# Who scales the sub-layer outputs by the inverse root: VectorE and GpSimd together, or VectorE alone

## The reference

```
x = x + 0.5 * rmsnorm(swiglu(rmsnorm(x, n[0]), w1_gu[l], w1_down[l]), n[1])      # q = 0
m, S_a, S_r = mixer(rmsnorm(x, n[2]), pos, w_in[l], ..., w_out[l], ...)
x = x + rmsnorm(m, n[3])                                                         # q = 1
x = x + 0.5 * rmsnorm(swiglu(rmsnorm(x, n[4]), w2_gu[l], w2_down[l]), n[5])      # q = 2

rmsnorm(x, g) = x * rsqrt(mean(x * x) + 1e-6) * g
```

## Time and profile before

| | us |
|---|---|
| three runs | 2445.9, 2448.19, 2452.44 |
| their median | 2448.19 |
| the profiled execution's own time | 2452.13 |
| its span, first to last instruction | 2450.3 |
| TensorE busy | 2334.9 (95%) |
| VectorE busy | 814.8 (33%) |
| ScalarE busy | 865.8 (35%) |
| GpSimd busy | 999.2 (41%) |

### The profile page before, as it was taken

One profiled execution on the slowest core, in us unless ns is written; L12 is line 12 of the kernel. 1 busy time (PEld: TensorE's weight loads), 2 busy tenths in 40 slices (PEclk: granted clock), 3 DMA queues, 4 the chain that ended last, 5 costly groups with the idle time before them and its releaser, 6 DMA issues.

```text
span 2450.3 us, 44621 instructions
## 1 busy us (share of the span) xinstructions
PE 2334.9 (95%) x17793; PEld 2260.2 (92%) x17793; DVE 814.8 (33%) x1065; ACT 865.8 (35%) x1396; POOL 999.2 (41%) x814
## 2 busy tenths in 40 slices
PE   8999999899989899999889999989998989999998
PEld 7999999799877899999879999988998779999997
DVE  4222200687434522210142221015864344222102
ACT  4333333442312433333343333334423234333322
POOL 3444444544113544444434444444442044444443
PEclk9999999899989999999989999999999899999999
DMA  5322232232304123322223332223223132222231
GB/s 159 90 86 86 73 90 75 73 87 63 94 24 120 53 86 89 91 71 87 76 70 87 90 89 74 84 67 87 78 70 80 40 103 69 86 86 86 78 88 60
DMA packets 382847, 198.44 MB, mean 81 GB/s; under 512 B 6853, under 2 KB 381401, under 8 KB 382617
## 3 DMA queue, kind: packets, MB, share of 16 engines
q1 hardware_dynamic: 355976, 182.18, 25.8%
q10 hardware_dynamic: 26768, 14.84, 2.2%
HBM read 187.68 MB, written 9.31 MB: 80 GB/s over the span
## 4 chain that ended last, share of the span: by engine, by line
issue 41%; PE 31%; POOL 23%; DVE 2%; POOLq 1%; ACT 0%; SPq 0%; DMA 0%; DVEq 0%; ACTq 0%
PE ps L489 28%; POOL w_lo L433 21%; PE ps L608 1%; POOL y_out L423 1%; POOL y L423 1%; DVE x_sq L1105 1%; POOLq L432 1%; DVE x L1150 0%; PE ps L690 0%; DVE q_lvl L1224 0%; PE ps L647 0%; PE ps L692 0%; PE ps L697 0%; DVE a_gla L1240 0%; PE ps L627 0%
## 5 line engine op out<-in xcount | busy, mean ns | idle before, releaser
L433 POOL TENSOR_TENSOR w_lo<-raw,w_hi 128x512 fp32r<-128x512 f32 (+3 forms) x768 | 942.2, 1232 | 1321.4 <-ACT w_hi L870 1319.2
L489 PE MATMUL ps<-xs_hi,w_hi 128*128 128x272 f32 x3744 | 791.2, 293 | 64.9 <-DVE xs_lo L1095 56.5
L870 ACT ACTIVATE w_hi<-raw 128x512 fp32r<-128x512 f32 (+3 forms) x768 | 436.1, 577 | 1027.9 <-PE ps L489 1016.6
L489 PE MATMUL ps<-xs_lo,w_hi 128*128 128x272 f32 x3744 | 780.2, 290 | 0.0
L489 PE MATMUL ps<-xs_hi,w_lo 128*128 128x272 f32 x3744 | 778.9, 289 | 0.0
L489 PEld LDWEIGHTS ps<-xs_hi,w_hi 128*128 128x128 f32 x3744 | 591.3, 190 | 75.6 <-DVE xs_lo L1095 61.6
L489 PEld LDWEIGHTS ps<-xs_lo,w_hi 128*128 128x128 f32 x3744 | 598.1, 191 | 0.0
L489 PEld LDWEIGHTS ps<-xs_hi,w_lo 128*128 128x128 f32 x3744 | 592.1, 190 | 0.0
L489 PE MATMUL ps<-h_hi,w_hi 128*128 128x272 f32 x1408 | 292.2, 289 | 0.0
L489 PE MATMUL ps<-h_lo,w_hi 128*128 128x272 f32 x1408 | 290.3, 287 | 0.0
L489 PE MATMUL ps<-h_hi,w_lo 128*128 128x272 f32 x1408 | 290.0, 287 | 0.0
(11 more groups left out here) (173 smaller groups left out, 1703.5 us busy)
## 6 DMA issues: line engine op xcount, KB each, us to landing
raw<-in_w_gu_dram SPq DMA_DIRECT2D x176, 512.0 KB, 3.8
raw<-in_w_in_dram SPq DMA_DIRECT2D x56, 512.0 KB, 3.8
raw<-in_w_down_dram SPq DMA_DIRECT2D x64, 384.0 KB, 3.2
raw<-in_w_down_dram SPq DMA_DIRECT2D x64, 320.0 KB, 3.1
raw<-in_w_out_dram SPq DMA_DIRECT2D x16, 512.0 KB, 3.7
ret_state<-in_state_ret_dram ACTq DMA_DIRECT2D x8, 512.0 KB, 6.0
out_dram<-ret_state ACTq DMA_DIRECT2D x8, 512.0 KB, 3.2
x_tok<-in_x_prompt_dram SPq DMA_DIRECT2D x4, 512.0 KB, 5.5
```

Of the source, the lines that this page charges most:

```text
L433: pool.tensor_tensor(w_lo[:, s, 0:n, :], raw[:, u, k0:k0 + n, :], w_hi[:, s, 0:n, :].bitcast(F32), ALU.subtract).then_inc(split_ready[s], 1)
L489: mm = pe.matmul(ps[:, bank + a, 0:HALF], w[:, s, k, :], v[:, kx, a * HALF:(a + 1) * HALF], start=(start and n == 0), stop=(stop and n == 2))
L870: act.activation(w_hi[:, s, 0:n, :], raw[:, u, k0:k0 + n, :], ACT.Copy).then_inc(hi_split, 1)
```

## The change

At every change of stage VectorE scales all eight tiles itself. GpSimd's program has no scale any more and only makes low parts of weights. The two tables of who scales what, the semaphore of GpSimd's scales and its function are gone. In VectorE's program the scale of tile k+1 is issued ahead of the addition of tile k.

```diff
-    DVE_SCALES = ((0, KD // 2), (0, KD // 2), (0, 1, 3, 5, 7))
-    POOL_SCALES = tuple(tuple(k for k in range(KD) if k not in own) for own in DVE_SCALES)
...
-        y_scaled = sig("y_scaled", sum(len(own) for own in DVE_SCALES))
-        y_scaled_pool = sig("y_scaled_pool", sum(len(own) for own in POOL_SCALES))
+        y_scaled = sig("y_scaled", 3 * KD)
...
-            def scale_y(l, q, ks):
-
-                wait(pool, post_ready, l, q)
-                for k in ks:
-                    if k in POOL_SCALES[q]:
-                        pool.tensor_tensor(y_tile(q, k), y_tile(q, k), acc[:, :], ALU.mult).then_inc(y_scaled_pool.sem, 1)
...
                 for f in range(2):
-                    group(l * GROUPS + UP[f], FULL_KT, PAIR_ORDER,
-                          before_unit={2: lambda: scale_y(l, 1, range(KD))} if f == 1 else {})
+                    group(l * GROUPS + UP[f], FULL_KT, PAIR_ORDER)
...
-                    if f == 1:
-                        scale_y(l, 2, range(KD))
                     if f == 0:
-                        group(l * GROUPS + WIN, ALO_KT, before_unit={2: lambda: scale_y(l, 0, range(KD // 2)),
-                                                                     3: lambda: scale_y(l, 0, range(KD // 2, KD))})
+                        group(l * GROUPS + WIN, ALO_KT)
...
             def residual(l, q, pre=None):
 
                 wait(dve, post_ready, l, q)
+
+                def scale_y(k):
+                    dve.tensor_tensor(y_tile(q, k), y_tile(q, k), acc[:, :], ALU.mult).then_inc(y_scaled.sem, 1)
+
+                scale_y(0)
                 for k in range(KD):
-                    yk, own = y_tile(q, k), k in DVE_SCALES[q]
-                    for n in ((0, 1) if k == 0 else (k + 1,)):
-                        if n in DVE_SCALES[q]:
-                            dve.tensor_tensor(y_tile(q, n), y_tile(q, n), acc[:, :], ALU.mult).then_inc(y_scaled.sem, 1)
+                    if k + 1 < KD:
+                        scale_y(k + 1)
                     if pre is not None and k >= 2:
                         pre_low(l, pre, k - 2)
-                    if own:
-                        wait(dve, y_scaled, l, nth_scale(DVE_SCALES, q, k))
-                    else:
-                        wait(dve, y_scaled_pool, l, nth_scale(POOL_SCALES, q, k))
+                    wait(dve, y_scaled, l, q * KD + k)
```

More of the change, by code:

```diff
@@ L335, in y_tile @@
             return (y_out if q == 1 else y)[:, k, :]
-        def nth_scale(table, q, k):
-            return sum(len(own) for own in table[:q]) + table[q].index(k)
         def ahead_of_wait(eng):
@@ L416, in _, with group @@
             pool.wait_ge(loaded, LOADS)
-            def scale_y(l, q, ks):
-                wait(pool, post_ready, l, q)
-                for k in ks:
-                    if k in POOL_SCALES[q]:
-                        pool.tensor_tensor(y_tile(q, k), y_tile(q, k), acc[:, :], ALU.mult).then_inc(y_scaled_pool.sem, 1)
-            def group(g, kts, order=UNIT_ORDER, before_unit={}):
+            def group(g, kts, order=UNIT_ORDER):
                 for i, (u, half) in enumerate(order):
-                    if half == 0:
-                        if u in before_unit:
-                            before_unit[u]()
                     _, k0, n = half_units(kts[u])[half]
@@ L1138, in residual @@
                 wait(dve, post_ready, l, q)
+                def scale_y(k):
+                    dve.tensor_tensor(y_tile(q, k), y_tile(q, k), acc[:, :], ALU.mult).then_inc(y_scaled.sem, 1)
+                scale_y(0)
                 for k in range(KD):
-                    yk, own = y_tile(q, k), k in DVE_SCALES[q]
-                    for n in ((0, 1) if k == 0 else (k + 1,)):
-                        if n in DVE_SCALES[q]:
-                            dve.tensor_tensor(y_tile(q, n), y_tile(q, n), acc[:, :], ALU.mult).then_inc(y_scaled.sem, 1)
+                    if k + 1 < KD:
+                        scale_y(k + 1)
                     if pre is not None and k >= 2:
                         pre_low(l, pre, k - 2)
-                    if own:
-                        wait(dve, y_scaled, l, nth_scale(DVE_SCALES, q, k))
-                    else:
-                        wait(dve, y_scaled_pool, l, nth_scale(POOL_SCALES, q, k))
-                    dve.scalar_tensor_tensor(out=x[:, k, :], in0=yk, scalar=post_gain(l, q, k), in1=x[:, k, :],
+                    wait(dve, y_scaled, l, q * KD + k)
+                    dve.scalar_tensor_tensor(out=x[:, k, :], in0=y_tile(q, k), scalar=post_gain(l, q, k), in1=x[:, k, :],
                                              op0=ALU.mult, op1=ALU.add).then_inc(x_ready.sem, 1)
```

## The result

| | before | after |
|---|---|---|
| runs of the first comparison, us | 2445.9, 2448.19, 2452.44, 2452.6 | 2425.64, 2427.81, 2430.42, 2430.53 |
| their median | 2450.32 | 2429.11 |
| ratio, 95% interval | | 0.9921 [0.9906, 0.9936] |
| second comparison, 17 and 6 runs: median | 2446.53 | 2430.08 |
| ratio, 95% interval | | 0.9930 [0.9916, 0.9943] |

The change makes the kernel 0.7 to 0.8% faster: 21.2 us by the first medians, 16.4 by the second. The forecast was 17.3 us and 2431 us.

The account below looks back on a forecast made before the run. TensorE bounds the kernel, idling at the changes of stage for VectorE's low parts of x. Gains of 6.2 + 8.4 + 1.4 + 1.3 = 17.3 us from 2448.19 give about 2431 us, range 2425 to 2441.

Parts of the forecast that it names:

- What bounds the kernel: Whole kernel: TensorE, whose movable idle time is 56.5 us at the changes of stage, waiting for VectorE's low parts of x.
- GpSimd's help is paid for by VectorE: Changes of stage: both engines together finish six instructions in 5.4 us, which VectorE alone would finish in about 4.
- The rival that GpSimd was not the cause: Changes of stage: VectorE's long instructions stay and the added scales come on top; 15 us slower, 2463 us; chance 0.04.
- q = 0: Change of stage q = 0, twice: VectorE's part takes 17.7 us, the sum of squares starts 3.1 us earlier; 6.2 us.
- q = 1: Change of stage q = 1, twice: no GpSimd instruction left, TensorE's 2.27 us wait goes; gain 4.2 us each, 8.4 us.
- q = 2 of layer 0: Change of stage there: sixteen VectorE instructions and four meetings take 14.9 us against 16.3; gain 1.4 us, bounds 0 and 5.6.
- the rule: q = 2 of layer 0: skill's whole-length exclusion of VectorE and reading GpSimd; each meeting costs up to 1.4 us, gain 0.
- The end: q = 2 of layer 1: last addition starts at 2441.0 instead of 2442.33; gain 1.3 us, bounds 1.0 and 1.5.
- The sum: Whole kernel: gains of 6.2, 8.4, 1.4 and 1.3 us make 17.3 us, so about 2431 us.
- The clock in part: q = 0 and q = 1: TensorE's lower clock takes part of the gain back, leaving 10.5 us, 2438 us; chance 0.15.
- The clock low through q = 1: q = 1: TensorE's clock stays at 1.2 GHz, 7 us lost each time with 100 slow matmuls, 2459 us; chance 0.03.
- Given back later: Later TensorE waits for low parts of weights or transfers: only the end's 1.3 us and a little stay, 2446 us; chance 0.06.

Follow-up runs that it names:

- the pair of busy runs: Kernel after, with GpSimd doing unused work where the scales stood: 30 multiplications that read, 2470.2 us; or memsets that only write, 2422.9 us.
- each third of the change: Kernel before, all eight scales on VectorE at one place only: ratio to before 0.9972 (q = 0), 0.9961 (q = 1), 0.9977 (q = 2).

## Why the prediction was right

*What bounds the kernel.* Right. The stages that were named moved, and the FFN stretches between them kept within 0.2 us what they had.

*GpSimd's help is paid for by VectorE.* Right, and shown rather than argued by the pair of busy runs: the same 1.85 us beside unrelated reads, 0.78 beside writes. The rival that GpSimd was not the cause is out: with GpSimd idle no instruction of q = 1 is longer than 0.79 us.

*q = 0.* Forecast 17.7 us of VectorE and 3.1 us gained, measured 17.5 and 3.4: the four meetings with small low parts cost 0.2 us each, not 0.28. (The forecast gives 4.2 us as this term's upper bound and 3.4 in the lower end of its range; 3.4 came.) TensorE still waits 1.0 us for the squares, and its first full tile started at 449.11 at the high clock, so the clock took nothing back. The new pattern, a k every 2 us, had all eight k's run at 1.2 GHz (the clock rose at about 448.8), but so had they before, until 452.2.

*q = 1.* Forecast 16.6 us of VectorE and 4.2 us gained, measured 16.7 and 3.8. TensorE's own work was done 25.2 us behind the first scale, as the forecast has it with one stretch at 1.2 GHz (25.3). The step that was a little off is the squares, taken at the 8.20 us of the earlier trace rows: they took 9.2. TensorE releases its slots sooner, so of the four large low parts of weights that are made here the last three start 2.2 us behind the first instead of 4.1, and all four fall beside the seven additions, where before the last one began only at their end (at 824.69 us in layer 0, where the squares of VectorE end at 825.31):

```profile
2012.35 9.16 DVE L1084 TENSOR_TENSOR x_sq<-x_sq 128x544 f32<-128x544 f32 x7
```

is layer 1's, against 8.19 us before. So the squares became the bound, 0.63 us behind TensorE's own work, and the stretches at the lower clock (granted 0.67 from 799 to 803 and 0.90 to 807) cost nothing. A TensorE that gets there sooner brings GpSimd's reads, which hold the squares up, forward with it.

*q = 2 of layer 0.* Forecast 14.9 us for the sixteen instructions with four meetings at 1.04; measured from 1208.98 to 1223.9, 14.9. An addition beside a large low part, after, and the scale behind it:

```profile
1212.67 1.78 DVE L1129 SCALAR_TENSOR_TENSOR x<-y,half_gain,x 128x544 f32<-128x544 f32 x1
1214.37 0.71 DVE L1120 TENSOR_TENSOR y<-y,acc 128x544 f32<-128x544 f32 x1
```

It costs 1.70 us from start to start, 1.0 more than alone, not GpSimd's whole 1.4 us, so the 1.4 us of gain that the forecast had from the rows came, and the one by the rule (0) did not. The two agree on who is held up and differ on how much. The loop's turn before the low parts of x shrank from 2.13 to 1.88 us. The stage as a whole gave 2.2 us, 0.3 of them in the loop's turn and 0.6 in the moment at which TensorE's clock rose (1225.77 is 8.7 us earlier than 1234.46, the squares 9.3). Those 0.9 us are luck: with all eight scales on VectorE at q = 2 alone both went the other way.

*The end.* Forecast 1.3, measured 1.1: the last addition starts 10.0 us after the first scale, as worked out, and the last transposes ran at the lower clock.

*The sum.* 17.3 us forecast, 17.7 us in the stages. The traces differ by 21.7, because the forecast's steps say nothing of the mixer, whose time is not the same in all kernels though its program is; the forecast had only the spread of the runs for it. Three runs of before were too few to see that the median lies near 2446.5 and that the profiled execution was one of the longest. The time forecast, 2431 us, is 1 to 2 us from the medians; the 16.4 and 21.2 us of the two comparisons, on either side of the 17.3, show how far medians of a few runs move.

*The rivals.* The clock in part: excluded at q = 0, without effect at q = 1. The clock low through q = 1: excluded. Given back later: excluded, since each third of the change kept its stage's gain.

## What to carry to other kernels

Where VectorE is what the next stage waits for, handing part of its two-input work to GpSimd can make it slower: compare VectorE's time from start to start with GpSimd reading and with GpSimd idle, and count six instructions together in 5.4 us against six alone in 4. GpSimd's memsets, which only write, cost it nothing here. Before a difference of two traces is explained, cut both into the same stages: here 4 of 22 us lay in a stage that the change did not touch.

## What the runs showed of the hardware

An instruction of VectorE with two SBUF inputs takes 1.70 to 1.78 us from start to start beside a reading instruction of GpSimd and 0.64 to 0.70 alone; beside a memset it stays at 0.70.

TensorE's granted clock fell to half for 12 us and more in which TensorE was busy without a break, among small matmuls, of at most 128 columns (0.50 from 692 to 704 us, 55 matmuls instead of 100). In the 4 us from 686 to 690, just before it fell, TensorE was busy for 3.4, and so it was in layer 1 from 1894 to 1898, where the clock stayed at 1.00. So idleness ahead of the stretch does not tell the two apart, and in the one trace with more unused matmuls at the waits ahead of it the stretch was there all the same. In the 15 us before layer 1, 48 more instructions of unused matmuls kept it at 1.00.
